# Norms and products in shared blocks, conditioning rows on plain products, and an expert loop over pairs of experts with GpSimd forming one remainder

## The reference, cut to what matters

```python
def rms_norm(x, g):
    return x * rsqrt(mean(x * x, -1) + 1e-6) * g
def adaln(cond, w_ada, b_ada):          # 1024 -> 6 * 1024, for two conditions
    return split(silu(cond) @ w_ada + b_ada, 6)
x = x + gt1 * (o @ w_out);  h = rms_norm(x, g) * (1 + sc2) + sh2
x = x + gt2 * ((silu(h @ w_gate) * (h @ w_up)) @ w_down)
# fourier part of the mixer: real part of a 2-d FFT over tokens and 64 channels
def moe_swiglu(h, router, w_gate, w_up, w_down):
    top_val, top_idx = top_k(h @ router, 2)
    gates = sum(one_hot(top_idx, 8) * softmax(top_val))
    for e in range(8):
        out = out + gates[:, e] * ((silu(h @ w_gate[e]) * (h @ w_up[e])) @ w_down[e])
```

## Time and profile before

| what | value |
| --- | --- |
| runs, median of 3 | 3140.36 us (3136.24 to 3140.94) |
| profiled execution | 3135.54 us, of it 3133.8 us span |
| mean granted clock of TensorE | 0.899 |
| PE busy | 2664.2 us, 85% |
| DVE busy | 1994.3 us, 64% |
| ACT busy | 1071.9 us, 34% |
| POOL busy | 201.4 us, 6% |
| read from HBM | 540.55 MB |

### The profile page before, as it was taken

One profiled execution on the slowest core, in us unless ns is written; L12 is line 12 of the kernel. 1 busy time (PEld: TensorE's weight loads), 2 busy tenths in 40 slices (PEclk: granted clock), 3 DMA queues, 4 the chain that ended last, 5 costly groups with the idle time before them and its releaser, 6 DMA issues. The chain is left out here.

```text
span 3133.8 us, 50194 instructions
## 1 busy us (share of the span) xinstructions
PE 2664.2 (85%) x18684; PEld 2400.9 (77%) x18684; DVE 1994.3 (64%) x3414; ACT 1071.9 (34%) x1804; POOL 201.4 (6%) x179
## 2 busy tenths in 40 slices
PE   7778898799776889686379966757999999999999
PEld 4667897699565779685379965547988988988988
DVE  6555776577764577755857744654666666666665
ACT  5333444344442444231134421221322322322322
POOL 0050000000004000061000040000000000000000
PEclk9889999899897999896589985577999999999999
DMA  9422352255562134340034440002877877877876
GB/s 354 172 81 82 130 187 106 88 185 190 192 231 76 69 144 184 126 149 14 0 122 181 173 146 1 1 32 91 320 277 274 318 276 277 317 276 277 319 272 224
DMA packets 57195, 543.16 MB, mean 173 GB/s; under 512 B 6584, under 2 KB 6904, under 8 KB 9080
## 3 DMA queue, kind: packets, MB, share of 16 engines
q1 hardware_dynamic: 53840, 529.55, 46.0%
q10 hardware_dynamic: 3248, 12.17, 1.1%
HBM read 540.55 MB, written 1.15 MB: 173 GB/s over the span
## 5 line engine op out<-in xcount | busy, mean ns | idle before, releaser
L2040 PEld LDWEIGHTS bank<-projc,ring 128*128 128x128 f32 x5632 | 654.6, 192 | 17.6 <-issue 4.5
L2040 PE MATMUL bank<-projc,ring 128*128 128x128 f32 x5632 | 655.8, 275 | 1.0 <-DVE projc L2122 1.0
L571 PE MATMUL bank<-src_hi,w_hi 128*128 128x256 f32 x1472 | 420.3, 286 | 29.4 <-DVE w_lo L844 28.2
L791 ACT ACTIVATE w_hi<-ring 128x1024 fp32r<-128x1024 f32 x264 | 278.7, 1059 | 419.8 <-PE bank L573 415.6
L572 PE MATMUL bank<-src_lo,w_hi 128*128 128x256 f32 x1472 | 419.2, 285 | 0.0
L573 PE MATMUL bank<-src_hi,w_lo 128*128 128x256 f32 x1472 | 418.9, 285 | 0.0
L844 DVE TENSOR_TENSOR w_lo<-ring,w_hi 128x1024 fp32r<-128x1024 f32 x264 | 321.7, 1220 | 100.3 <-ACT w_hi L791 99.0
L571 PE MATMUL bank<-w_hi,src_hi 128*128 128x256 f32 x896 | 268.6, 300 | 77.8 <-DVE w_lo L700 69.0
L571 PE MATMUL bank<-w_hi,act_hi 128*128 128x512 f32 x704 | 292.8, 416 | 23.5 <-DVE w_lo L844 12.5
L571 PEld LDWEIGHTS bank<-src_hi,w_hi 128*128 128x128 f32 x1472 | 285.0, 194 | 35.4 <-DVE w_lo L844 30.3
L572 PEld LDWEIGHTS bank<-src_lo,w_hi 128*128 128x128 f32 x1472 | 285.2, 194 | 3.1
(11 more groups left out here) (335 smaller groups left out, 4212.5 us busy)
## 6 DMA issues: line engine op xcount, KB each, us to landing
ring<-in_moe SPq DMA_DIRECT2D x176, 1536.0 KB, 8.4
ring<-in_ffn SPq DMA_DIRECT2D x66, 1536.0 KB, 6.4
ring<-in_w_ada SPq DMA_DIRECT2D x48, 1024.0 KB, 4.9
ring<-in_ffn_ev SPq DMA_DIRECT2D x22, 1536.0 KB, 6.4
ring<-in_w_in SPq DMA_DIRECT2D x18, 1024.0 KB, 4.8
ring<-in_w_out SPq DMA_DIRECT2D x12, 1024.0 KB, 4.8
ring<-in_ev_in SPq DMA_DIRECT2D x12, 1024.0 KB, 4.8
ring<-in_od_in SPq DMA_DIRECT2D x7, 1024.0 KB, 4.7
```

Of the source, the lines that this page charges most:

```text
L571: pe.matmul(out, ah, bh, start=start and i == 0, stop=False, skip_group_check=True)
L791: act.activation(p.wH[:, kind, :], piece(c, kind), ACT.Copy).then_inc(p.w_hi[kind].sem, 1)
L2040: mm = pe.matmul(p.ps[2 + k % 2][:, u * P:u * P + P], w[:, kt, :], hJ[:, k // FC, kt, :], start=kt == 0, stop=kt == KT - 1)
```

## The change

1. `norm_src`, `turn` and `fourier` ahead of a product become the opening of the product's own block (`Normed`, `Turned`). ACT and DVE split the first two weight pieces inside it, the source tiles are kept by DVE and ACT by turns, and PE starts with the first source tile that is ready. The norm between the two blocks of layers (`g_final`) joins the norm after it. `turn`'s result is split straight from PSUM.
2. `adaln` drops the split: PE multiplies the ring's float32 pieces by a source widened to 32 columns, four row blocks going to four different groups of 32 output partitions; ACT and DVE copy the results, and PE sums the four groups in small matmuls.
3. `moe`: gate and up become split products (source 128 tokens as the stationary side, 256 weight columns moving), silu is formed by tanh, the activations are transposed on PE, there are two sets of `w_hi`/`w_lo`, the work between two jobs is spread over the chunks of the neighbouring jobs, and the loop runs over a pair of jobs, written out, with the first and the last job outside. DVE forms the remainders of the gate and up pieces, POOL that of the down piece. The norm's gain is multiplied by POOL into `xn` beside `route`. The transfer of a chunk is two, sides and down.

```diff
 def linear(p, front, n_tok, ...):
+            (normed_act if is_norm else turned_act)(p, act, front, high, front_loads)
+            for q in range(2, 2 * n):
...
+            (normed_pe if is_norm else turned_pe)(p, pe, front)
+            for i, k in enumerate(front.order):
+                if k // 4 not in [j // 4 for j in front.order[:i]]:
+                    pe.wait_ge(*p.w_lo[k // 4](1))
+                pe.wait_ge(*src_ready(front.ready[i]))
+                for m in range(2):
+                    mm = product(0, k, m, i == 0, i == KT - 1)
 def normed_dve(p, dve, f, split):
+    dve.tensor_scalar(p.xn[:, 0, :], f.rows[:, 0, :], st[:, 0:1], None, ALU.mult).then_inc(normed.sem, 1)
+    split(0)
+    for j in (0, 2):
+        dve.wait_ge(*turned(j + 1))
+        for k in (2 * j, 2 * j + 1):
+            dve.tensor_scalar(h[:, k, :], ...).then_inc(kept_v.sem, 1)
+    for k in range(4):
+        low(k)
+    split(1)
+    for k in range(4, KT):
+        low(k)
 def adaln(p, l, loads):
-            for q in range(2 * n):
-                mm = products(pe, p.ps[c % 2][0:2, 0:PC], ...)
+            for c in range(n):
+                p.wait_chunk(pe, g0 + c)
+                for k in range(KT):
+                    j = k % 4
+                    mm = pe.matmul(p.ps[c % 4][32 * j:32 * j + 32, 0:PC], wide[:, k, :], w[:, k, :],
+                                   start=k < 4, stop=k >= 4)
 def moe(p):
-            def up(i, turn, k):
-                for u in range(2):
-                    w = piece(k, u).rearrange("p (k f) -> p k f", k=KT)
-                    for kt in range(KT):
-                        mm = pe.matmul(p.ps[2 + k % 2][:, u * P:u * P + P], w[:, kt, :], hJ[:, k // FC, kt, :], ...)
+            def up(i, k):
+                for half in range(2):
+                    pe.wait_ge(*at(p.w_lo[half], i, k + 1))
+                    mm = products(pe, p.ps[2 + k % 2][:, 0:2 * P],
+                                  [((p.srcH[:, 4 * half + q, hs], p.srcL[:, 4 * half + q, hs]),
+                                    (wh[:, q, :], wl[:, q, :])) for q in range(4)], half == 0, half == 1)
+            def turn_act(i, k, early):
+                pe.wait_ge(*at(a_ready, i, k + 1))
+                pe.transpose(p.ps[4][:, 0:P], aJ[:, k % 2, :], p.ident[:, :]).then_inc(a_turned.sem, 1)
+        @block.gpsimd
+        def _(pool):
+            def step(i, b, r, first, last):
+                m = b * FC + r - 2
+                if there(r, 2, first):
+                    wh, wl = [v[:, DOWN, :] for v in sets[m % 2]]
+                    pool.wait_ge(*at(p.w_hi[DOWN], i, m + 1))
+                    pool.tensor_tensor(wl, down_piece(m), wh.bitcast(F32), ALU.subtract).then_inc(p.w_lo[DOWN].sem, 1)
 # ACT, step of chunk k: high of piece 0 | tanh(k-2) | high of piece 1 | activations(k-3) | high of down(k-2)
```

More of the change, by code:

```diff
@@ new lines, with __init__, h_tiles @@
+class Turned:
+    def __init__(self, groups, mix=None):
+        self.groups, self.mix = groups, mix
+        ks = [k0 + i for sources, k0 in groups for i in range(len(sources) // NT)]
+        self.order = tuple(ks) + (() if mix is None else (3, 4))
+        counts = [j + 1 for j, (sources, _) in enumerate(groups) for _ in range(len(sources) // NT)]
+        self.ready = tuple(counts) + (() if mix is None else (len(groups) + 1, len(groups) + 2))
+def h_tiles(p):
+    return p.work[:, 0:KT * T].rearrange("p (k t) -> p k t", k=KT)
@@ new lines, in turned_tiles, with turned_act @@
+def turned_tiles(p, f, j):
+    sources, k0 = f.groups[j]
+    n = len(sources) // NT
+    return (p.ps[4 + j][:, 0:n * T].rearrange("p (k t) -> p k t", k=n), p.srcH[:, k0:k0 + n, :],
+            p.srcL[:, k0:k0 + n, :])
+def turned_act(p, act, f, split, loads=()):
+    turned, hi = p.sig("x_turned"), p.sig("src_hi_ready")
+    seq_done, seq_kept, out_done = mix_signals(p)
+    split(0)
+    for j in range(len(f.groups)):
+        act.wait_ge(*turned(j + 1))
+        bank, high, low = turned_tiles(p, f, j)
+        act.activation(high, bank, ACT.Copy).then_inc(hi.sem, 1)
+        if j == 0:
+            split(1)
+    if f.mix is not None:
+        for c in range(2):
+            act.wait_ge(*out_done(c + 1))
+            act.activation(p.srcH[:, 3 + c, :], p.ps[2 + c][:, 0:T], ACT.Copy).then_inc(hi.sem, 1)
@@ new lines, in front_begins, with front_passed @@
+def front_begins(p, f):
+    f.root0 = p.rstd.base
+def front_passed(p, f):
+    normed, squared, turned, kept_v, kept_a, hi, lo, final = front_signals(p)
+    if isinstance(f, Normed):
+        normed.passed(NT)
+        squared.passed(f.stats)
+        final.passed(NT if f.final is not None else 0)
+        kept_v.passed(4)
+        kept_a.passed(4)
+        turned.passed(4)
+    else:
+        turned.passed(len(f.groups))
+        if f.mix is not None:
+            for s in mix_signals(p):
+                s.passed(2)
+    hi.passed(f.ready[-1])
+    lo.passed(f.ready[-1])
@@ L616, in side_product, with linear @@
     return mm
-def linear(p, src, n_tok, n_feat=0, out=None, out_feat=None, residual=None, gate=None, side=None,
-           out_at=None, loads=(), beside=None):
+def linear(p, front, n_tok, n_feat=0, out=None, out_feat=None, residual=None, gate=None, side=None,
+           out_at=None, loads=(), front_loads=(), beside=None, split=False):
     nc = p.nc
@@ L646, in _, with high @@
         def _(act):
[L647 to L651 removed]
+            def high(q):
                 g, b = g0 + q // 2, q % 3
@@ L1985, in moe, with there @@
+    def there(r, lag, first):
+        return r - lag < FC and not (first and r < lag)
     with nc.Block(no_gpsimd_drain=True) as block:
@@ new lines, in _, with step @@
+            for part in range(2):
+                keep_job(0, 0, part)
+            walk(act, between, step)
+        @block.gpsimd
+        def _(pool):
+            between = pool.value_load(p.trip[0:1, 1:2], min_val=3, max_val=7)
+            def step(i, b, r, first, last):
+                m = b * FC + r - 2
+                if there(r, 2, first):
+                    wh, wl = [v[:, DOWN, :] for v in sets[m % 2]]
+                    pool.wait_ge(*at(p.w_hi[DOWN], i, m + 1))
+                    pool.tensor_tensor(wl, down_piece(m), wh.bitcast(F32), ALU.subtract).then_inc(p.w_lo[DOWN].sem, 1)
+            walk(pool, between, step)
```

959 lines of the change are left out of this document (532 added, 427 removed).

## The result

| | before | after |
|---|---|---|
| median of four runs, us | 3139.45 | 3060.57 (3059.27 to 3063.31) |
| span of the profiled execution, us | 3133.8 | 3057.2 |

A forecast was written before the change was run, and what follows sets the result against it. It took PE to bound the products, after a gap at each entry, and the expert loop. Savings of 98 (entries), 22 (conditioning) and 49 (experts), 169 us, took 3135.5 to 2966.5, as a median 2971; range 2905 to 3058.

The forecast's parts named there:

- The gap: At norm entries, PE's wait between its transposes and the first product: 6.8 us before, estimated 0.7 after, 61 us over ten.
- The cover: At norm entries, splitting both first weight pieces while PE waits for the norm or transposes for 3.67 us.
- a tail of 2 each: At each conditioning stage's end, two more matmuls and an addition before the last gate rows' write: 2 us lost.
- Rival (a): Conditioning matmuls run one after another, not side by side: 43 us less gain, 3014 us; chance 0.18.
- my three cases: Expert chunk cycle by what POOL's operation covers of DVE's work: 4.8 us for 0.6, 5.1 for 0.3, 5.5 for nothing.
- The step between jobs: In the experts, DVE's additions, low parts and pick matrices: up to 5.4 us a job, partly under POOL, taken as 3.6.
- The exclusion of GpSimd and VectorE: In the experts, DVE's remainders and POOL's operation hold each other up: at least 4.46 us a chunk; 4.95 taken.
- the sign that I gave against it: An expert chunk staying under 4.7 us would show that DVE and POOL's mutual blocking does not bind.
- Rival (b): POOL's expert operation blocks nobody; PE bounds at 104.6 us a job, 112 saved, 2908 us; chance 0.11.
- Rival (c): POOL's expert operation covers nothing and DVE's extra work adds up: 126.4 us a job, 62 lost, 3082 us; chance 0.08.
- The combination of (a) and (d): Serial conditioning matmuls together with entries giving back half their gain: near 3055 us, within the chance left over.
- (d): Entries give half their gain back, as POOL's work or a later wait ends last: 49 us, 3020 us; chance 0.10.

The follow-up runs named there:

- e8: On a kernel with later additions and no GpSimd in the experts, the first two weight pieces' splits moved behind the norm's steps in ten entries: 2937.73 us.
- e6: The kernel before with only the changed conditioning stage, all eight products of a chunk in one column group instead of four: 3179.20 us, ratio 1.0142.
- e1: The changed kernel with VectorE's four scatter additions one chunk later, in steps 6 to 9 of the next job instead of 5 to 8: 2952.41 us.
- e2: e1 with the down piece's remainder formed by VectorE as well, so GpSimd has no work in the expert part: 2887.71 us, ratio 0.9200.
- e3: e1 with GpSimd forming only 16 of 1024 columns of the down piece's remainder from the third expert chunk on, so results differ: 2898.27 us.
- e10: e3 with GpSimd making ten subtractions of 16 columns one after another, 160 of 1024 columns in all: 2900.36 us, ratio 0.9245.

## Why the prediction missed, point by point

**Part 1, forecast 98, measured 114.** Right in mechanism. The gap is 0.66 where I had 0.7, the final norm 12.4 us where I had about 13, and the output product shown has no gap. A feed-forward, which has one entry, is 7.4 to 8.2 us shorter where I had 6.1. The cover is 5.0 of that (e8); how the rest divides between the boundary and a clock that is up sooner, no run tells. Ten entries of 1.3 to 2.1 more than forecast are 13 to 21 us, about the 16 between 98 and 114.

**Part 2, forecast 22, measured 27.** Right in mechanism, and its price for four groups side by side, 0.9 us for eight products, holds at the clock at which it was read (1.07 with the last one's own duration). What it left out is that the clock would be at the lower level for most of the stage, where they take 1.93; and it left out the sums of columns (0.99 there), so a chunk takes 3.03 in such stretches (33.10 to 36.13), not 2.83. The other way, the transfers were faster than the 370 GB/s that I took as full speed (415 in 12 to 50). The stages gained 9.0 and 18.4, for which I had 9.4 and 17 less a tail of 2 each; no run shows that tail. Rival (a) did not come. Its price left out the sums too: one after another is 45 us slower than before (e6), not 21.

**Part 3, forecast a gain of 49, measured a loss of 64.** Here the prediction failed, by 113 us, and in one step of it: "DVE's four additions, two low parts and four pick matrices [...] are up to 5.4; a part lies under POOL's operations; I take 3.6". It counted busy time and never asked when each addition's bank is there. The order of the queues would have told: TensorE's scatter stands behind a `down` that needs what VectorE makes right before the addition. The wait is 28 x 4.1 = 115 us in seven jobs, and e1, which moves nothing else, gives 108 back. With it gone the sum of the part comes out: e1 has 113.5 us a job, forecast 112.5, and its expert stretch is 979.4 us against 1024.5, 45 gained of 49 forecast. The total of e1, 2952, lies 19 below the forecast by what parts 1 and 2 gave more.

That agreement is partly luck, since three errors meet in it. A chunk away from the additions takes 4.65, not 4.95: in e1 GpSimd's operation covers VectorE's second product and low part, the best of my three cases (4.8). The step between jobs is 5 to 8 us in the jobs without a jump (107.9 to 111.0), not 3.6: TensorE's gathers did not disappear into spare time, the two chunks that hold them take 6.1. And what is lost at jumps back, some 13 us each in e1 and 10.1 in e2, was not in the sum.

**The exclusion of GpSimd and VectorE** holds (e3, e10), although the sign that I gave against it, a chunk under 4.7, came up: 4.65 comes from the good cover, not from want of the exclusion. But I drew too little from it: it made the experts slower than a version without GpSimd by 65 us, since VectorE had room for the third remainder. "Without that rule PE would be the bound and a job 104.6": e2, with VectorE alone, is at 102.8 between jumps. Rival (b)'s time was to be had by using less of GpSimd, not by its blocking nobody. **Rival (c)**, no cover, came near the measured time (3082) by another mechanism: its mark, 5.5 us for every chunk, is not in the profile, which has 4.6 for most and 8 to 10 for four in each job. The combination of (a) and (d) came nearer still: I put it near 3055, though its prices add up to 2971 + 43 + 49 = 3063. Neither of the two happened, so that is luck as well.

## What to carry to other kernels

When a consumer is spread over an in-order queue, price its wait, not its duration: write down for each item what stands ahead of its producer on the producer's queue, and whether any of that waits for the consumer's own step. If it does, put it one step later: here that was worth 108 us, and the later additions waited for nothing. Before handing work to GpSimd beside a busy VectorE, compare VectorE's time with both: three remainders at 1.22 cost it no more than two at 1.85. And before comparing two durations on TensorE, compare the granted clock of the two stretches: the same eight products are 1.07 us in one place and 1.93 in another.

## What the runs showed of the hardware that was not expected

- Float32 products of 32 outputs in four column groups ran side by side: eight took 1.07 us against 3.64 in one group, both at clock 1.00, and a set of four took 0.22 from start to start where a single record in one group took 0.23.
- With the shorter products the clock stayed at the lower level: with waits for transfers between them TensorE's records lasted 0.63 us from 12 to 50 us; with one group, busy almost throughout, 0.38 from 20 us on.
- Ten subtractions of 16 columns on GpSimd, 2 to 3 us together, left VectorE's remainders at 1.25 us; one of 1024 columns, of the same duration, brought their mean to 1.85.
- A jump back in a loop of 44 chunks cost 10.1 us in e2 and some 13 in e1, with TensorE idle in e2 for up to 5.3 of it with no releaser.
